# Depthwise weights behind the first outputs, urgency carried over table changes, and cross weights fetched later

## The chip, the cores and the metric

The program runs on the 8 NeuronCores of one Trainium2 chip; each core has TensorE (PE), VectorE (DVE), ScalarE (ACT), GpSimd (POOL) and SyncE (SP). The metric is the device time of the slowest core in microseconds. The input has 4 sequences of 4096 tokens; a core takes 2048 tokens of one sequence and 128 tokens ahead of them, the halo. There is no traffic between the cores.

## The reference, cut to what matters

```python
h = rmsnorm(x, norm_g)
(q, k, v, g_attn, u_conv, g_conv, q_cross, g_cross, merge) = split(h @ w_in)
a = sliding_window_attention(q, k, v, positions, attn_sinks)     # window 128, 8 heads
y_attn = (a * silu(g_attn)) @ w_o_attn
c = conformer_conv(u_conv, ...)       # GLU, causal depthwise conv of width 31, LayerNorm, silu
y_conv = (c * silu(g_conv)) @ w_pw + b_pw
m = memory_cross_attention(q_cross, rmsnorm(mem), w_mem_kv)      # 256 memory tokens, 4 heads
y_cross = (m * silu(g_cross)) @ w_o_cross
gates = sigmoid(merge)                # three gates per channel
x = x + (gates0 * y_attn + gates1 * y_conv + gates2 * y_cross) @ w_out
return rmsnorm(x, final_norm_g)
```

## The kernel before, in words

The 2048 tokens are four groups of 512 (tg 0 to 3) and sixteen blocks of 128 (B). Activations lie channel-major in SBUF, so most matmuls are 128x128 by 128x512, eight of them (k-chunks) to one projected unit of 128 channels. PSUM has eight banks of 512 float32.

**Stages.** (1) *Start*: x of group 0 arrives in eight chunks `xs0_0` to `xs0_7`. For each chunk ACT squares it and DVE multiplies it with the gain (`raw`, 128x512, bf16 out). Between the chunks DVE builds the attention's bias tiles from the positions (`bias_ops`, 128x128 operations). Then `rms_stats`, `rms_apply` (eight 128x512 scalar-tensor-tensor operations on DVE), and the units `u_k_raw`, four `u_q_raw` and `u_v`; DVE multiplies or copies each out of PSUM. (2) *Attention*, sixteen steps of a block: `scores` (banks 0 to 3, then four Exp on ACT), `att_l` (bank 5), `att_o` (bank 4), `att_r` (DVE, Ln and Exp on ACT, a 128x512 multiply on POOL), `att_g` (DVE, which empties bank 4). Each step has some projection units beside it (`fill`); a unit takes the next bank of `pj`, and must wait until what was in that bank has been read. (3) `glu_halo`, then the convolution stage: `glu` of group 0, `u_gc`, and per group `conv(c)` for c 0 to 3 with `glu` of the next group between them. `conv` reads `Rt`, a copy of the GLU result `aT` shifted per tap, written by 16 DMAs of SP per half group (`relayout(tg, cp)`: cp 0 serves conv 0 and 1, cp 1 serves conv 2 and 3). It also reads `Lw`, the depthwise weights spread on a diagonal, which POOL builds in 16 operations of 128x256 (`lw_part`). (4) Cross attention: `x_scores`, `x_attend`, `x_out`; its weights `w_qc` and `w_gx` come by two POOL DMAs of 1 MB each (bf16 in SBUF), first used when conv of the last group runs. (5) Merge and output projection.

**What sets the order.** `Prog.add` records every operation with reads and writes, a busy time, and for ACT the activation table. `Prog.plan` then makes each engine's order: PE and SP keep program order; ACT, DVE and POOL take, among the next 48, what can start first, and of those equally early the one with the least `due`. Due times go backwards from PE's. On ACT only operations of the current table group may be taken. Every engine runs its list in order, and waits for semaphores; an operation that waits holds up all behind it on its engine. DMAs of SP are "hardware_dynamic" in the profile, those of POOL "software_dynamic".

Since each helper issues its operation in one line, the profile's lines are those of helpers: L527 and L531 are matmuls (L531 the tiled ones of attention and convolution), L551 activations, L555 tensor-tensor, L566 and L569 tensor-scalar with one and two operations, L576 scalar-tensor-tensor, L580 copies, L588 DMAs.

Of the kernel before, what the change touches and what calls it, by code (L numbers as in the profile page):

```python
# [8 lines left out]
ALU = mybir.AluOpType  # L9
# [69 lines left out]
class Prog:  # L79
# [3 lines left out]
    RATE = {(True, False): (300e3, 0.0), (False, True): (0.0, 330e3), (True, True): (60e3, 260e3)}  # L83
# [70 lines left out]
    def plan(self):  # L154
# [14 lines left out]
        for op in reversed(ops):  # L169
            if op.eng != "pe":  # L170
                m = t + 10.0
                for u in users[op.idx]:
                    m = min(m, due[u])
                due[op.idx] = m - op.late - self.HOP - (2.0 if op.sem is not None else 0.0)
# [11 lines left out]
        free = {e: 5.0 for e in queue}  # L186
# [204 lines left out]
def build_program():  # L391
# [274 lines left out]
    def lw_part(cg):  # L666
        tt("pool", Lw[:, cg * 8:(cg + 1) * 8, :], E32.unsqueeze(1).to_broadcast([128, 8, 32]),
           consts[:, C_WR + cg * 8:C_WR + (cg + 1) * 8].unsqueeze(2).to_broadcast([128, 8, 32]), ALU.mult)
# [390 lines left out]
    def halo_stats():  # L1059
# [18 lines left out]
        [V(1), GA(1, 0), GA(1, 1), ST(2), AP(2, 0, 8)],  # L1078
# [3 lines left out]
        [V(2), GA(2, 0), GA(2, 1), load_conv],  # L1082
        [GA(2, 2), GA(2, 3), K(3), MQ(0, 8)],
# [3 lines left out]
        [GA(3, 3), MK(0), MK(1)],  # L1087
# [3 lines left out]
    pj[0] = [6, 7, 3]  # L1091
    for n in range(18):
        pjn[0] = 0
# [7 lines left out]
        first = 2 if n in (1, 5, 9) else 1  # L1101
        for f in here[:first]:
            f()
# [16 lines left out]
    glu(0, 0)  # L1120
    glu(0, 1)
# [9 lines left out]
    for tg in range(NTG):  # L1131
        nx = tg + 1
        for c in range(4):
            conv(c)
            if nx < NTG:
                glu(nx, c)
                if c % 2 == 1:
                    relayout(nx, c // 2)
            elif c < 2:
                u_qc(0, 2 * c)  # L1140
                u_qc(0, 2 * c + 1)
            else:
                u_gx(0, 2 * c - 4)
                u_gx(0, 2 * c - 3)
# [195 lines left out]
```

How the kernel before makes its waits and increments, by code:

```python
            def run(engname, e):  # L309
                seen = {}
                for i in order.get(engname, ()):
                    op = ops[i]
                    need = {}
                    for d in op.deps:
                        p = ops[d]
                        s = p.sem if p.sem is not None else p.eng
                        if p.sigval > need.get(s, 0):
                            need[s] = p.sigval
                    for s, v in need.items():
                        if seen.get(s, 0) >= v:
                            continue
                        e.wait_ge(sems[s], v)
                        seen[s] = v
                    ins = op.emit(e)
                    if op.signal:
                        s = op.sem if op.sem is not None else op.eng
                        ins.then_inc(sems[s], op.inc)
                if engname == "sp":
                    for fi in final_waits:
                        p = ops[fi]
                        s = p.sem
                        if seen.get(s, 0) < p.sigval:
                            e.wait_ge(sems[s], p.sigval)
                            seen[s] = p.sigval
```

## Time and profile before

| | before |
|---|---|
| median of 3 runs | 705.59 us (682.0 to 705.97) |
| the profiled execution | 681.28 us; span 679.7 us on core 4, the slowest; the eight cores 675.8 to 679.7 us |
| PE busy | 633.7 us, 93% |
| DVE, ACT, POOL busy | 347.7, 290.2, 121.6 us |
| DMA | 58.56 MB; software_dynamic 27.79 MB, hardware_dynamic 29.79 MB |

How to read it: nearly the whole span is PE work. What is not is found in PE's timeline, where an idle time stands in brackets in front of the instruction that ended it, with the engine that released it. A number behind "x" is a count. "PEclk" is the TensorE clock that was granted, as a share of 2.4 GHz; 0.50 is 1.2 GHz.

### The profile page before, as it was taken

The page shows a single profiled execution, that of the slowest core. Times are in us where ns is not written, and L with a number is a line of the kernel's source. Part 1 is how long each engine was busy: PE and PEld are TensorE (multiplying, and loading weights), DVE is VectorE, ACT ScalarE, POOL GpSimd, SP SyncE. Part 2 cuts the span into 40 slices and gives each one's busy share as a digit, 9 for nine tenths or more (in the row PEclk, how much of TensorE's full clock was granted, in tenths as well). Part 3 has the DMA queues.
Part 4 walks back from the last instruction along what each step waited for, and adds up shares of the span by engine and source line. Part 5 has one row for each costly group of instructions (what it writes and reads, how often), then busy time and mean ns, then how long its engine had stood idle before and what let it go on. Part 6 is the DMA issues. An engine that isn't in the chain of part 4 may idle for free.

```text
span 679.7 us, 11202 instructions; the slowest of 8 cores (675.8 to 679.7 us)
## 1 busy us (share of the span) xinstructions
PE 633.7 (93%) x3537; PEld 282.2 (42%) x3600; DVE 347.7 (51%) x570; ACT 290.2 (43%) x506; POOL 121.6 (18%) x155
## 2 busy tenths in 40 slices
PE   2499999997999999997999999999999999999994
PEld 0144434443444444443444444444444444444442
DVE  5989677754135453555565333344444343444336
ACT  4058865563236373657778322222222212222224
POOL 5301222121000000012322411122111222122210
PEclk9999999997999999998999999999999999999998
DMA  7895797005534233479900770210031002500003
GB/s 168 123 243 150 123 123 141 1 2 86 121 86 96 61 72 79 109 130 159 172 14 1 97 89 2 94 63 31 32 120 66 32 31 91 189 31 32 32 0 155
DMA packets 28281, 58.56 MB, mean 86 GB/s; under 512 B 3648, under 2 KB 17216, under 8 KB 26432
## 3 DMA queue, kind: packets, MB, share of 16 engines
q0 software_dynamic: 8624, 27.79, 23.4%
q1 hardware_dynamic: 19456, 29.79, 15.9%
q8 instruction: 31, 0.51, 0.3%
q14 instruction: 26, 0.21, 0.1%
q10 hardware_dynamic: 144, 0.26, 0.1%
HBM read 62.09 MB, written 8.39 MB: 104 GB/s over the span
## 4 chain that ended last, share of the span: by engine, by line
PE 84%; DVE 5%; issue 4%; ACT 3%; DMA 2%; SPq 2%; DVEq 0%; ACTq 0%
PE psum L527 75%; PE psum L531 9%; ACT arena L551 2%; DVE arena L555 2%; SPq L588 2%; DVE arena L566 2%; DVE arena L576 1%; DMA arena<-xT 1%; ACT L551 1%; DMA arena<-arena 0%; DVE arena L580 0%; DVE arena L569 0%; DVEq L322 0%; ACTq L322 0%; SPq L322 0%
## 5 line engine op out<-in xcount | busy, mean ns | idle before, releaser
L527 PE MATMUL psum<-arena 128*128 128x512 bf16 (+3 forms) x2705 | 570.3, 367 | 32.5 <-ACT arena L551 17.2
L527 PEld LDWEIGHTS psum<-arena 128*128 128x128 bf16 x2768 | 259.0, 98 | 342.9 <-issue 59.8
L551 ACT ACTIVATE arena<-psum 128x512 bf16<-128x512 f32 (+1 forms) x244 | 137.7, 597 | 231.8 <-PE psum L527 158.3
L555 DVE TENSOR_TENSOR arena<-psum,arena 128x512 f32<-128x512 f32 (+2 forms) x143 | 105.2, 745 | 133.1 <-PE psum L527 90.8
L555 POOL TENSOR_TENSOR arena<-arena 128x512 f32<-128x512 f32 (+3 forms) x95 | 96.3, 1020 | 282.5 <-DVE arena L576 152.8
L551 ACT ACTIVATE arena<-arena 128x512 f32<-128x512 f32 (+7 forms) x174 | 106.9, 643 | 91.2 <-DVE arena L555 71.0
L531 PE MATMUL psum<-arena 128*32 128x512 bf16 (+3 forms) x832 | 67.3, 383 | 4.5 <-DVE arena L555 2.4
L576 DVE SCALAR_TENSOR_TENSOR arena<-psum,arena 128x512 f32<-128x512 f32 (+2 forms) x52 | 37.0, 712 | 58.6 <-PE psum L527 55.4
L576 DVE SCALAR_TENSOR_TENSOR arena<-arena 128x512 bf16<-128x512 f32 (+4 forms) x79 | 60.8, 806 | 11.1 <-ACT arena L551 10.2
L580 DVE CAST arena<-psum 128x512 bf16<-128x512 f32 (+2 forms) x70 | 46.0, 660 | 35.1 <-PE psum L527 35.0
L551 ACT ACTIVATE arena<-psum,arena 128x512 bf16<-128x512 f32 (+4 forms) x58 | 35.7, 649 | 52.7 <-PE psum L531 31.4
L555 DVE TENSOR_TENSOR arena<-arena 128x512 bf16<-128x512 f32 (+3 forms) x78 | 44.6, 588 | 14.6 <-ACT arena L551 10.8
L531 PEld LDWEIGHTS psum<-arena 128*32 128x32 bf16 (+3 forms) x832 | 23.2, 99 | 45.1 <-issue 31.8
L588 POOL DMA_DIRECT2D arena<-win x11 | 6.1, 558 | 161.3 <-issue 124.9
L566 DVE TENSOR_SCALAR arena<-psum,arena 128x512 f32<-128x512 f32 x16 | 12.0, 751 | 39.2 <-ACT arena L551 38.1
L566 DVE TENSOR_SCALAR arena<-arena 128x128 bf16<-128x128 f32 (+5 forms) x58 | 22.4, 434 | 4.0 <-DMA arena<-xT 3.4
L551 ACT ACT_TABLE_LOAD x13 | 16.7, 1283 | 10.4 <-DVE arena L555 5.2
L569 DVE TENSOR_SCALAR arena<-arena 128x512 f32<-128x512 f32 (+3 forms) x33 | 10.9, 339 | 14.9 <-ACT arena L551 13.2
L555 DVE TENSOR_TENSOR arena<-arena,psum 128x512 f32<-128x512 f32 x16 | 10.3, 682 | 8.7 <-PE psum L527 8.7
L576 DVE SCALAR_TENSOR_TENSOR arena<-arena,psum 128x512 f32<-128x512 bf16 x16 | 11.0, 685 | 6.6 <-PE psum L527 5.3
L588 POOL DMA_DIRECT2D out<-arena x12 | 7.5, 626 | 28.6 <-DVE arena L576 26.6
L569 POOL TENSOR_SCALAR arena<-arena 128x1 f32<-128x1 f32 x12 | 2.3, 188 | 50.9 <-ACT arena L551 50.9
(14 smaller groups left out, 13.9 us busy)
## 6 DMA issues: line engine op xcount, KB each, us to landing
arena<-win POOLq DMA_DIRECT2D x11, 1024.0 KB, 16.0
arena<-xT SPq DMA_DIRECT2D x32, 256.0 KB, 7.8
arena<-xtok SPq DMA_DIRECT2D x16, 512.0 KB, 4.3
arena<-arena SPq DMA_DIRECT2D x96, 67.5 KB, 2.0
out<-arena POOLq DMA_DIRECT2D x12, 512.0 KB, 3.0
arena<-wo POOLq DMA_DIRECT2D x3, 1024.0 KB, 22.7
arena<-arena SPq DMA_DIRECT2D x32, 67.4 KB, 2.0
arena<-wqg POOLq DMA_DIRECT2D x4, 512.0 KB, 11.8
```

Of the source, the lines that this page charges most:

```text
L527: P.add("pe", lambda e: e.matmul(out, lhsT=lhsT, rhs=rhs, start=start, stop=stop), reads=[lhsT, rhs], writes=[out], busy=max(0.000421 * wi ...
L531: P.add("pe", lambda e: e.matmul(out, lhsT=lhsT, rhs=rhs, start=start, stop=stop, tile_position=tile_position), reads=[lhsT, rhs], writes= ...
L551: P.add("act", lambda e: e.activation(out=out, in_=in_, func=func, **kw), reads=rd, writes=wr, busy=0.06 + 0.00085 * width(out), lag=0.12, ...
L555: P.add(eng, lambda e: e.tensor_tensor(out=out, in0=in0, in1=in1, op=op), reads=[in0, in1], writes=[out], busy=vcost(eng, "tt", out, in_ps ...
L566: P.add(eng, lambda e: e.tensor_scalar(out=out, in0=in0, scalar1=s1, scalar2=None, op0=op0), reads=rd, writes=[out], busy=cost)
L569: P.add(eng, lambda e: e.tensor_scalar(out=out, in0=in0, scalar1=s1, scalar2=s2, op0=op0, op1=op1), reads=rd, writes=[out], busy=cost)
L576: P.add(eng, lambda e: e.scalar_tensor_tensor(out=out, in0=in0, scalar=scalar, in1=in1, op0=op0, op1=op1), reads=rd, writes=[out], busy=vc ...
L580: P.add(eng, lambda e: e.tensor_copy(out=out, in_=in_), reads=[in_], writes=[out], busy=vcost(eng, "copy", out, in_psum(in_)))
L588: P.add(eng, lambda e: e.dma_start(out=out, in_=in_), reads=[in_] + list(after), writes=[out], dsem=sem, final=final, busy=0.7 if eng == " ...
```

## The change

What it does:

- `lw_part` gets a read of the attention result of a block, so that it can only run after `att_g` of that block; the calls go from "one in each of steps 0 to 15" to steps 2 to 15 and two behind the loop.
- `plan`: the due time of an ACT operation is also bounded by the earliest due time of the next table group (`close`); SP is free from 6.5 instead of 5.0; the shares of bandwidth that it assumes for the two kinds of DMA (`RATE`) change.
- The units of the attention steps take banks 6 and 7 in turn, with no reset per step; before 6, 7 and 3, from 6 anew in each step. Some units are written in another order (`fill`).
- `att_o(15)` and `att_g(15)` come behind `glu(0, 0)`; `pjn` is set to 0 ahead of `glu_halo` alone, so the halo's four units take banks 6, 7, 0, 1 and `glu(0, 0)` takes 2 and 3. Before it was set to 0 again behind the halo, and `glu(0, 0)` took 6 and 7.
- The DMAs of `w_qc` and `w_gx` are issued after `conv(0)` of group 0 has written `cbf[:, 0, :]`; before ahead of `glu(0, 0)`.

```diff
-    RATE = {(True, False): (300e3, 0.0), (False, True): (0.0, 330e3), (True, True): (60e3, 260e3)}
+    RATE = {(True, False): (360e3, 0.0), (False, True): (0.0, 330e3), (True, True): (200e3, 160e3)}
...
+        close = {}
+        for op in reversed(ops):
+            if op.eng != "pe":
+                m = t + 10.0
+                for u in users[op.idx]:
+                    m = min(m, due[u])
+                due[op.idx] = m - op.late - self.HOP - (2.0 if op.sem is not None else 0.0)
+                if op.eng == "act":
+                    r = group[op.idx]
+                    due[op.idx] = min(due[op.idx], close.get(r + 1, m) - 1.3 - op.busy)
+                    close[r] = min(close.get(r, m), due[op.idx])
...
-        free = {e: 5.0 for e in queue}
+        free = {e: 6.5 if e == "sp" else 5.0 for e in queue}
...
-    def lw_part(cg):
...
+    def lw_part(cg, after):
+        e8 = E32.unsqueeze(1).to_broadcast([128, 8, 32])
...
+        P.add("pool", lambda e: e.tensor_tensor(out=out, in0=e8, in1=w8, op=ALU.mult), reads=[e8, w8, after], writes=[out],
+              busy=0.65)
...
-        [V(1), GA(1, 0), GA(1, 1), ST(2), AP(2, 0, 8)],
+        [GA(1, 0), V(1), GA(1, 1), ST(2), AP(2, 0, 8)],
...
-    pj[0] = [6, 7, 3]
-    for n in range(18):
-        pjn[0] = 0
+    pj[0] = [6, 7]
+    for n in range(17):
...
-        if n < 16:
-            lw_part(n)
+        if 2 <= n < 16:
+            lw_part(n - 2, part(gA, blocks[n - 2]))
...
-        if n == 16:
-            pj[0] = [6, 7, 0, 1, 2, 3]
-            glu_halo()
-
-    dma("pool", w_qc, win_d[3], "w3")
-    dma("pool", w_gx, win_d[4], "w4")
+    lw_part(14, part(gA, 13))
+    lw_part(15, part(gA, 13))
+    pj[0] = [6, 7, 0, 1, 2, 3]
+    pjn[0] = 0
+    glu_halo()
     glu(0, 0)
+    att_o(15)
+    att_g(15)
     glu(0, 1)
...
         for c in range(4):
             conv(c)
+            if tg == 0 and c == 0:
+                dma("pool", w_qc, win_d[3], "w3", after=[cbf[:, 0, :]])
+                dma("pool", w_gx, win_d[4], "w4")
```

**POOL's queue at the start.** The 128x256 operations are `lw_part`, the 128x512 ones `att_r`. Before:

```order
L588 DMA arena<-wkv 128x2048
L555 TENSOR_TENSOR arena<-arena 128x256 x10
L588 DMA arena<-wqg 128x2048 x4
L555 TENSOR_TENSOR arena<-arena 128x256 x5
L555 TENSOR_TENSOR arena<-arena 128x512 x2
L588 DMA arena<-wmem 128x8x512
```

and with the change:

```order
L593 DMA arena<-wkv 128x2048
L593 DMA arena<-wqg 128x2048 x4
L560 TENSOR_TENSOR arena<-arena 128x512
L675 TENSOR_TENSOR arena<-arena 128x256
L560 TENSOR_TENSOR arena<-arena 128x512
L675 TENSOR_TENSOR arena<-arena 128x256
L593 DMA arena<-wmem 128x8x512
```

No `lw_part` is left between the DMAs of the first weights; they stand among the multiplies of `att_r`. On DVE, 75 operations stood ahead of the first one of `rms_apply(0)` and 91 ahead of the last `u_q_raw(0)`; now 63 and 82: bias operations (128x128) that went behind.

**PE's queue from the last attention steps to the convolution.** The 128x30 rows are `glu_halo`, the four 64x512 behind them `att_o(15)`. Before:

```order
L531 MATMUL psum<-arena 64x512 x8
L527 MATMUL psum<-arena 128x30 x64
L531 MATMUL psum<-arena 64x512 x4
L527 MATMUL psum<-arena 128x512 x96
L531 MATMUL psum<-arena 32x512 x32
```

and with the change:

```order
L536 MATMUL psum<-arena 64x512 x8
L532 MATMUL psum<-arena 128x30 x64
L532 MATMUL psum<-arena 128x512 x16
L536 MATMUL psum<-arena 64x512 x4
L532 MATMUL psum<-arena 128x512 x80
L536 MATMUL psum<-arena 32x512 x32
```

`att_o(15)` went behind the sixteen matmuls of `glu(0, 0)`.

**DVE's queue where the last LayerNorm meets the first cross attention.** The x2 and x3 rows and the single arena<-arena ones are `ln_norm` (second step) and `ln_gate` of group 3, the CAST rows copy `u_qc` units, the L576 or L581 rows are `x_attend`. Before:

```order
L580 CAST arena<-psum 128x512
L555 TENSOR_TENSOR arena<-arena 128x512 x2
L580 CAST arena<-psum 128x512
L555 TENSOR_TENSOR arena<-arena 128x512 x2
L580 CAST arena<-psum 128x512
L576 SCALAR_TENSOR_TENSOR arena<-arena,psum 128x512
L555 TENSOR_TENSOR arena<-arena 128x512 x2
L580 CAST arena<-psum 128x512
L555 TENSOR_TENSOR arena<-arena 128x512
```

and with the change:

```order
L585 CAST arena<-psum 128x512
L560 TENSOR_TENSOR arena<-arena 128x512 x3
L585 CAST arena<-psum 128x512
L560 TENSOR_TENSOR arena<-arena 128x512
L585 CAST arena<-psum 128x512
L581 SCALAR_TENSOR_TENSOR arena<-arena,psum 128x512
L560 TENSOR_TENSOR arena<-arena 128x512 x3
```

The x2 behind the first copy was `ln_norm(1)` and `ln_gate(0)`, with `ln_norm(2)` in the next pair and `ln_norm(3)` in the third; the x3 is now `ln_norm(1)`, `(2)` and `(3)`, ahead of every `ln_gate`. In POOL's and SP's queues the two cross weights and the relayouts keep their places; what changes is what the first of the two weight DMAs waits for.

## Rows read from the trace of the kernel before

**Rows 1.** Page, part 1: busy us, share, instructions.

```profile
PE 633.7 (93%) x3537; PEld 282.2 (42%) x3600; DVE 347.7 (51%) x570; ACT 290.2 (43%) x506; POOL 121.6 (18%) x155
```

**Rows 2.** PE timeline: start, busy us, count, in brackets the idle time before.

```profile
26.38 0.58 PE L527 MATMUL psum<-arena 128*128 128x512 bf16 x1 [6.70 <-DVE arena L566]
...
41.05 0.61 PE L531 MATMUL psum<-arena 64*128 64x512 bf16 x4 [0.74 <-DVE arena L555]
```

**Rows 3.** Windows: length, busy of PE, PEld, DVE, ACT, POOL, clock, DMA.

```profile
10.20:22.50 12.30, 6.53 (x12) 1.33 (x12) 12.20 (x20) 5.96 (x10) 12.14 (x20) 1.00 0.69 162
22.50:31.70 9.20, 4.24 (x9) 1.28 (x10) 8.88 (x42) 0.00 (x0) 0.01 (x1) 1.00 0.99 149
```

**Rows 4.** Windows, columns as in rows 3.

```profile
60.00:153.00 93.00, 90.40 (x629) 40.32 (x636) 65.52 (x106) 61.11 (x117) 19.79 (x20) 1.00 0.52 80
...
159.90:165.10 5.20, 5.19 (x13) 1.88 (x13) 2.59 (x10) 0.98 (x2) 0.00 (x0) 0.50 0.86 132
...
314.60:320.00 5.40, 5.29 (x16) 1.99 (x17) 1.53 (x3) 3.62 (x7) 2.31 (x2) 0.68 0.97 152
```

**Rows 5.** PE timeline around `glu_halo` and `glu(0, 0)`.

```profile
156.31 0.62 PE L531 MATMUL psum<-arena 128*64 128x512 bf16 x4 [1.19 <-DVE arena L555]
159.91 23.36 PE L527 MATMUL psum<-arena 128*128 128x512 bf16 x94 [2.98 <-ACT arena L551]
```

**Rows 6.** Chain of waits, time and length of each step, `conv(0)` and `conv(2)`, group 0.

```profile
181.22 3.35 DMA arena<-arena
...
184.71 1.89 PE psum L531 x29
...
195.56 1.61 PE psum L531 x25
```

**Rows 7.** PE timeline where the cross attention starts.

```profile
314.60 7.73 PE L527 MATMUL psum<-arena 128*128 128x512 bf16 x26 [3.34 <-ACT arena L551]
```

**Rows 8.** DVE timeline (as rows 2): `ln_gate(2)` and the last `ln_norm(3)` of group 3.

```profile
310.62 1.02 DVE L555 TENSOR_TENSOR arena<-arena 128x512 bf16<-128x512 bf16 x2
```

**Rows 9.** ACT timeline where the cross attention starts.

```profile
312.56 1.28 ACT L551 ACT_TABLE_LOAD   x1
```

**Rows 10.** DVE timeline around the start.

```profile
31.75 5.38 DVE L576 SCALAR_TENSOR_TENSOR arena<-arena 128x512 bf16<-128x512 f32 x8
...
46.68 1.67 DVE L566 TENSOR_SCALAR arena<-arena 128x512 bf16<-128x512 f32 x4
```

**Rows 11.** POOL timeline and the wqg tile: its four DMAs, issue to landing.

```profile
17.40 2.20 POOL L588 DMA_DIRECT2D arena<-wqg  x4
...
DMA to landing us min/median/max: 7.0/11.8/16.6
```

**Rows 12.** DMA view, 196 to 198 us: issues, KB each, us to landing.

```profile
arena<-arena SPq DMA_DIRECT2D x2, 67.5 KB, 2.1
```

**Rows 13.** ACT timeline: `csq` and `cbf` of `conv(0)`, group 0.

```profile
186.70 1.27 ACT L551 ACTIVATE arena<-psum,arena 128x512 bf16<-128x512 f32 x2 [2.73 <-PE psum L531]
```

**Rows 14.** SP timeline: the sixteen DMAs of `relayout(0, 1)`.

```profile
182.03 11.40 SPq L588 DMA_DIRECT2D arena<-arena  x16
```

**Rows 15.** DMA view, 171.5 to 173.5 us: packets by queue, then issues.

```profile
q0 software_dynamic: 53, 0.43, 103.8%
...
arena<-arena SPq DMA_DIRECT2D x2, 67.5 KB, 3.8
```

**Rows 16.** The `out` tile: a store issued at 508.1, then one at 546.0 us.

```profile
DMA to landing us min/median/max: 5.4/5.4/5.4
...
DMA to landing us min/median/max: 3.0/3.0/3.0
```

**Rows 17.** The win tile (durations in ns) and the DMA view in slices of 0.4 us, 158 to 174.

```profile
L588 POOL DMA_DIRECT2D arena<-win x2: 538/566/594, 158.2 to 158.8; - x2
...
DMA to landing us min/median/max: 10.3/13.1/16.0
...
DMA  0000000593994999686999999999989839899894
```

More of the change, by code:

```diff
@@ L168, in plan @@
                 t += op.busy
[L169 to L174, printed above, removed]
         group = {}
@@ L664, in build_program @@
     dma("pool", w_ga[1], wqg_d[3], "w_ga1")
-    def lw_part(cg):
-        tt("pool", Lw[:, cg * 8:(cg + 1) * 8, :], E32.unsqueeze(1).to_broadcast([128, 8, 32]),
-           consts[:, C_WR + cg * 8:C_WR + (cg + 1) * 8].unsqueeze(2).to_broadcast([128, 8, 32]), ALU.mult)
+    def lw_part(cg, after):
+        e8 = E32.unsqueeze(1).to_broadcast([128, 8, 32])
+        w8 = consts[:, C_WR + cg * 8:C_WR + (cg + 1) * 8].unsqueeze(2).to_broadcast([128, 8, 32])
+        out = Lw[:, cg * 8:(cg + 1) * 8, :]
+        P.add("pool", lambda e: e.tensor_tensor(out=out, in0=e8, in1=w8, op=ALU.mult), reads=[e8, w8, after], writes=[out],
+              busy=0.65)
     ts("dve", hb2, ccol(C_BGLU + 4, 4), 0.5, ALU.mult)
@@ L1081, in build_program @@
         [Q(2, 2), Q(2, 3), ST(3), AP(3, 0, 8)],
-        [V(2), GA(2, 0), GA(2, 1), load_conv],
-        [GA(2, 2), GA(2, 3), K(3), MQ(0, 8)],
+        [GA(2, 0), V(2), GA(2, 1), load_conv],
+        [GA(2, 2), K(3), GA(2, 3), MQ(0, 8)],
         [Q(3, 0), mem_stats, Q(3, 1), Q(3, 2)],
@@ L1086, in build_program @@
         [GA(3, 1), lambda: normed(memn, memT, C_GM, rm), GA(3, 2)],
-        [GA(3, 3), MK(0), MK(1)],
+        [MK(0), GA(3, 3), MK(1)],
         [MK(2), MK(3), MV(0)],
@@ L1100, in build_program @@
             scores(blocks[n])
-        first = 2 if n in (1, 5, 9) else 1
-        for f in here[:first]:
+        for f in here:
             f()
@@ L1107, in build_program @@
             att_g(blocks[n - 2])
-        for f in here[first:]:
-            f()
-        if n < 16:
-            lw_part(n)
+        if 2 <= n < 16:
+            lw_part(n - 2, part(gA, blocks[n - 2]))
         if n == 14:
             clear_pads()
-        if n == 16:
-            pj[0] = [6, 7, 0, 1, 2, 3]
-            glu_halo()
-    dma("pool", w_qc, win_d[3], "w3")
-    dma("pool", w_gx, win_d[4], "w4")
+    lw_part(14, part(gA, 13))
[3 more added lines that the diff above has]
+    glu_halo()
     glu(0, 0)
+    att_o(15)
+    att_g(15)
     glu(0, 1)
```

## The prediction

> **What bounds the kernel now.** The page's first part says that PE is busy for 93% of the span [rows 1], and the change takes no matmul away; so I read PE's timeline for the idle times, and for each the chain of waits back to what was late. Five places matter. In all of them PE stands while a queue in a fixed order is behind.
>
> *Start.* PE waits 6.70 us until 26.38 for DVE's `raw` chunks, and `scores(1)` begins its second half at 41.05, again behind DVE [rows 2]. From 10.2 to 31.7 DVE is busy throughout, but while POOL runs `lw_part` it gets through 20 instructions in 12.30 us, and afterwards through 42 in 9.20 us [rows 3]. So this stretch is bound by DVE, and DVE is held by POOL.
>
> *Attention.* From 60 to 153 PE is busy 90.40 of 93 us; DVE has 27 us to spare, POOL 73 [rows 4].
>
> *GLU.* PE stands from 155.12 to 156.31 and then 2.98 us until 159.91 [rows 5]. The second wait is for bank 6, which the halo's first unit still holds. Then the matmuls run at a granted clock of 0.50, 1.2 GHz, until 165.10 [rows 4].
>
> *Convolution.* `conv(0)` starts at 184.71, released by the last relayout DMA [rows 6].
>
> *Cross attention.* PE waits 3.34 us for ACT until 314.60 [rows 7], and the next 5.40 us have a mean clock of 0.68 [rows 4]. The last `ln_norm` on DVE is in the pair from 310.62 [rows 8]; its activation and a table load of 1.28 us [rows 9] have to pass before the Exp.
>
> **The change, part by part.** The sum goes against the profiled execution, 681.28 us (span 679.7 and 1.6 around it). The median of the three runs shown is 705.59, 24.3 above it; their lowest, 682.0, agrees with it.
>
> 1. `lw_part` leaves the start. Free of POOL, DVE takes (9.20 - 4 x 0.42)/38 = 0.20 us for a 128x128 operation, with 0.42 for a 128x512 one from 1.67/4 [rows 3, 10]. The 20 held instructions (4 wide, 16 narrow, by this window's shapes) would take 4.9 instead of 12.3: 7.4 us less. Nine narrow operations go behind the last `u_q_raw`: 1.8 less. The four weight DMAs of POOL remain, 2.20 us of issue [rows 11], and fall into the same stretch; they can hold DVE for 0 to 2.2, I take 1.3. Result 7.9 us. Is anything else late next? These DMAs follow w_kv directly, about 3 us earlier than now; `w_q0` lands 7.0 after its issue at 17.40 [rows 11], at 24.4, so in the change at about 21.5, when `u_k_raw` (from 17.8, eight matmuls at 0.43) ends. x of group 1 moves by 3 us too and PE by 8, which uses up slack, perhaps 0.5. The eight `rms_apply`, 5.38 us [rows 10], stay. **-7.9** (bounds -10 and 0, if the DMAs decide).
>
> 2. Attention. The fifteen remaining `lw_part` of interest now hold DVE about 0.4 us each (12.30/20 less 0.20), 6 us of DVE's 27 spare. Each reads `gA`, so it can hold POOL, and behind it the next `att_r` multiply and `att_g`, only if `att_g` is late; one step lies between. Two banks instead of three: in a step of three units the third waits until the first is read, one unit of 1.7 us later; the Exp of a gate unit on ACT, behind four score Exps, is the slow one. Bank 3 no longer holds up `scores`. Together **+1.5** (bounds -1.5, half of PE's 2.6 idle, and +14, 1 us a step). SP's new 6.5 and the bandwidth shares act only in the plan: 0.
>
> 3. GLU. Halo matmuls end at 155.12; `glu(0, 0)` in banks 2 and 3 needs 16 x 0.216 = 3.5, `att_o(15)` 0.6: 159.2. Bank 6 was read at 159.91 even behind the stall, and bank 7 needs one more such read before it is wanted, eight matmuls later. Allowing 0.3, `glu(0, 1)` starts at 159.5 instead of 165.8 (159.91, 5.2 at half speed and four more matmuls). **-6.3** (bounds -3.7, if the clock falls anyway, and -6.6).
>
> 4. `relayout(0, 0)` no longer meets weights. The chain has 3.35 us from its last issue to `conv(0)` [rows 6], against a landing of 2.1 in quiet [rows 12]. **-0.6** (0 to -1.1).
>
> 5. Cross weights behind `cbf` of `conv(0)`. This is the large term. `cbf` is written at 187.97 [rows 13], and the sixteen DMAs of `relayout(0, 1)`, which `conv(2)` needs, are issued from 182.03 to 193.43, one in 0.66 to 0.71 [rows 14]. So the weights are issued with some eight of them still to come; their packets begin 2.8 us after issue, and relayout packets about 1.2 after theirs, so the last five or six arrive behind two megabytes. What happens then stands in the trace: three relayout DMAs were issued before 173.5 with the weights still moving, and from 171.5 to 173.5 all 53 packets were the weights' [rows 15]; they landed after 3.8 us instead of 2.1 [rows 12]. The reverse is seen too: a POOL store issued behind three SP loads lands after 5.4 us, one alone after 3.0 [rows 16]. What comes first is served first. The second weight, issued 0.6 after the first, lands 16.0 later: 16.6 us from the first issue, of which 2.8 pass before the first packet and 1.2 behind the last one, as for a relayout; that leaves 12.6 us of packets [rows 17]. Counted from C, the start of `conv(0)`: `cbf` C+3.3, first weight packet C+6.3, last C+18.8, remaining relayouts landed C+20.5. `conv(2)` is due at C+10.85 [rows 6]: a wait of 9.7. The clock then falls as after the wait at 159.91: 5.2/2 less matmuls already run, 2.2. **+11.9** (bounds 0, and +14.5). `relayout(1, 0)` is late next, but `conv(0)` of group 1 is 19.4 us behind `conv(2)`.
>
> The Trainium skill, "DMA: Bandwidth & Descriptors", section Queues, rings and completion order, says an engine takes turns between queue rows packet by packet, a packet being some 9 to 17 descriptors. The 2 us without a relayout packet agree with that only if a whole weight DMA is one packet. By that rule the relayouts would get a turn between the two weights; that is rival B.
>
> 6. Urgency over table changes. `ln_norm(2)` and `(3)` follow `(1)` directly (306.5 to 307.7), four Silu of 0.8 end at about 309.6, the table load at 310.9 [rows 9], one Exp at 311.5; PE is there at 311.26 (314.60 - 3.34) [rows 7]. The wait shrinks from 3.34 to 0.3, and the low clock goes: (1 - 0.68) x 5.40 = 1.7 [rows 4]. **-4.7** (bounds 0 and -5.0).
>
> Sum: -7.9 + 1.5 - 6.3 - 0.6 + 11.9 - 4.7 = -6.1, so 675.2.
>
> **The rivals.**
>
> A (forecast), chance 0.50: 675.2, from 669 to 682 by the small terms.
>
> B, 0.15: the relayouts slip in between the two weights. Then they wait for one, 6.3 us less, and the clock may hold, 1 less: 668. For it: two separate DMAs. Against it: five relayouts of four descriptors per DMA engine need several turns.
>
> C, 0.15: no hold-up. Small packets interleave with the weights, or the last relayouts are out before them: 675.2 - 11.9 = 663.3. For it: at 173.5 the weights' rest was short, so a long hold-up is not seen. Against it: the served-first rows [rows 15, 16].
>
> D, the other side, 0.10: the attention steps pay for two banks and for POOL. Place: the third unit of a step, on PE, behind DVE's copy and ACT's Exp of the first. From 0.6 us a step this eats the forecast's gain (14 steps, 8 us); at 1 us it gives 675.2 - 1.5 + 14 = 687.7, and with the low clock after larger waits up to 696. For it: DVE is 70% busy there and gets 6 us more. Against it: before, PE lost only 2.6 us there.
>
> E, 0.08: the start does not get shorter, as first weights and x bound it: 683. For it: DMA share 0.99 from 22.5 [rows 3].
>
> 0.02 is left for something else.
>
> **The numbers.** Predicted 675. The cases reach from 663 (C) to 688 (D) with 0.9 of the chance. An execution like the two runs at 705.6 to 706.0 would put the forecast at 675 x 1.036 = 699; no row prices that difference and a median may lie there, so the high end is 700; for an execution like the profiled one the range is 662 to 688. Faster by over 2% is below 667.7, on equal footing: C, half of B and a little of A, 0.28. Slower by over 2%, above 694.9: the far end of D and what is left, 0.04. Within 2% (about what a measurement of this kernel can tell from no change): 0.68.
>
> **What would show it.** (1) Half of `scores(1)` at about 33 instead of 41.05. (2) PE idle over 0.5 us in attention at few steps. (3) `glu(0, 0)` directly behind the halo, clock 1.00. (5) A wait of some 9.7 us before `conv(2)` of group 0, released by a relayout DMA with a landing time over 10 us, then a clock of 0.50. Without it the forecast is wrong by its largest term and C holds. (6) No wait over 1 us between `x_scores(0)` and `x_scores(2)`. The forecast is also wrong if the first weights land no earlier.

## The result: 0.4% faster

| | before | changed |
|---|---|---|
| median of 6 runs | 694.03 us (681.68 to 795.22) | 678.85 us (677.0 to 679.52) |
| ratio of the times | | 0.9957, 95% interval 0.9942 to 0.9971 |
| profiled execution, span of the slowest core | 679.7 us | 677.8 us (the cores 671.1 to 677.8) |

The medians differ by more than the ratio, since some runs of the kernel before were disturbed; the ratio leaves those out. It is a gain of 2.9 us, 2 to 4 by the interval. The time forecast was 675 (675.2 in its sum). Against the profiled execution of before that was a gain of 6.1 us, twice what came.

**Where it came from and went.** From the traces of all eight cores the start of each unit's first weight load was read; the table has the median of the cores, in us, and the difference to before.

| start of | before | changed | difference | forecast so far |
|---|---|---|---|---|
| scores(1) | 39.5 | 31.1 | -8.4 | -7.9 |
| last u_q_raw of group 1 | 64.9 | 60.3 | -4.6 | |
| glu_halo | 152.9 | 146.9 | -6.0 | -6.4 |
| glu(0, 3) | 171.3 | 159.7 | -11.6 | -12.7 |
| conv(2), group 0 | 193.4 | 181.9 | -11.5 | -13.3 |
| conv(3), group 0 | 198.8 | 201.3 | +2.4 | -1.4 |
| x_scores(0) | 300.2 | 302.8 | +2.6 | -1.4 |
| x_scores(3) | 317.0 | 315.2 | -1.8 | -6.1 |
| end of the span | 677.2 | 675.4 | -1.8 | -6.1 |

So 11.5 us were won by conv(2) of group 0, 13.9 lost there, and 4.4 won in the cross attention. These are two single executions, and their 1.8 is not the 2.9 of the ratio; the table is for the places, the ratio for the total.

### The profile page after: what moved, and what is told of

It reads as the page before. It is cut to its first block, busy times and chain, and to the rows that moved or that the text cites. A ratio compares the mean times of both kernels' runs of the same rounds, so it can differ in the third digit from the quotient of the medians.

```text
span 677.8 us, 11291 instructions; the slowest of 8 cores (671.1 to 677.8 us)
## 1 busy us (share of the span) xinstructions
PE 635.3 (94%) x3600; PEld 280.2 (41%) x3600; DVE 344.9 (51%) x570; ACT 289.4 (43%) x506; POOL 122.7 (18%) x155
## 4 chain that ended last, share of the span: by engine, by line
PE 76%; DMA 6%; DVE 6%; SPq 4%; issue 4%; ACT 2%; POOL 1%; DVEq 0%; ACTq 0%; POOLq 0%
PE psum L532 70%; PE psum L536 7%; SPq L593 4%; DVE arena L581 3%; DMA arena<-xT 2%; DMA arena<-arena 2%; DMA arena<-wqg 2%; DVE arena L560 2%; ACT arena L556 2%; DVE arena L585 1%; POOL arena L560 1%; ACT L556 0%; POOL arena L593 0%; DVEq L327 0%; DVE arena L574 0%
## 5 line engine op out<-in xcount | busy, mean ns | idle before, releaser
L532 PE MATMUL psum<-arena 128*128 128x512 bf16 (+2 forms) x2768 | 571.3, 366 | 20.9 <-ACT arena L556 14.5
L560 POOL TENSOR_TENSOR arena<-arena 128x512 f32<-128x512 f32 (+2 forms) x79 | 85.1, 1078 | 250.6 <-DVE arena L581 185.5
L581 DVE SCALAR_TENSOR_TENSOR arena<-arena 128x512 bf16<-128x512 f32 (+4 forms) x79 | 65.4, 864 | 6.5 <-ACT arena L556 5.2
L581 DVE SCALAR_TENSOR_TENSOR arena<-psum,arena 128x512 f32<-128x512 f32 (+2 forms) x52 | 37.0, 712 | 58.1 <-PE psum L532 54.6
L560 DVE TENSOR_TENSOR arena<-arena 128x512 bf16<-128x512 f32 (+3 forms) x78 | 43.3, 571 | 12.7 <-ACT arena L556 9.2
L571 DVE TENSOR_SCALAR arena<-arena 128x128 bf16<-128x128 f32 (+5 forms) x58 | 16.9, 334 | 9.0 <-DMA arena<-xT 8.2
L675 POOL TENSOR_TENSOR arena<-arena 128x256 bf16<-128x256 bf16 x16 | 12.0, 756 | 24.8 <-DVE arena L560 24.7
L574 DVE TENSOR_SCALAR arena<-arena 128x512 f32<-128x512 f32 (+3 forms) x33 | 10.1, 316 | 11.8 <-ACT arena L556 10.1
L560 DVE TENSOR_TENSOR arena<-arena,psum 128x512 f32<-128x512 f32 x16 | 10.3, 679 | 8.7 <-PE psum L532 8.7
L581 DVE SCALAR_TENSOR_TENSOR arena<-arena,psum 128x512 f32<-128x512 bf16 x16 | 10.9, 684 | 4.2 <-PE psum L532 2.8
## 6 DMA issues: line engine op xcount, KB each, us to landing
arena<-wqg POOLq DMA_DIRECT2D x4, 512.0 KB, 12.3
```

The source lines that it names most:

```text
L532: P.add("pe", lambda e: e.matmul(out, lhsT=lhsT, rhs=rhs, start=start, stop=stop), reads=[lhsT, rhs], writes=[out], busy=max(0.000421 * wi ...
L560: P.add(eng, lambda e: e.tensor_tensor(out=out, in0=in0, in1=in1, op=op), reads=[in0, in1], writes=[out], busy=vcost(eng, "tt", out, in_ps ...
L571: P.add(eng, lambda e: e.tensor_scalar(out=out, in0=in0, scalar1=s1, scalar2=None, op0=op0), reads=rd, writes=[out], busy=cost)
L574: P.add(eng, lambda e: e.tensor_scalar(out=out, in0=in0, scalar1=s1, scalar2=s2, op0=op0, op1=op1), reads=rd, writes=[out], busy=cost)
L581: P.add(eng, lambda e: e.scalar_tensor_tensor(out=out, in0=in0, scalar=scalar, in1=in1, op0=op0, op1=op1), reads=rd, writes=[out], busy=vc ...
L675: P.add("pool", lambda e: e.tensor_tensor(out=out, in0=e8, in1=w8, op=ALU.mult), reads=[e8, w8, after], writes=[out], busy=0.65)
```

## The profile of the changed kernel

The page's first part and four windows, columns as in [rows 3]; core 6, the slowest, as in every view of this kernel here.

```profile
PE 635.3 (94%) x3600; PEld 280.2 (41%) x3600; DVE 344.9 (51%) x570; ACT 289.4 (43%) x506; POOL 122.7 (18%) x155
```

```profile
10.20:22.50 12.30, 8.19 (x18) 2.04 (x18) 12.19 (x51) 5.40 (x9) 2.76 (x5) 1.00 1.00 204
22.50:31.70 9.20, 9.16 (x73) 4.84 (x73) 8.87 (x23) 0.00 (x0) 0.00 (x0) 1.00 1.00 175
60.00:153.00 93.00, 89.65 (x680) 40.13 (x680) 66.93 (x100) 58.50 (x111) 30.45 (x35) 1.00 0.46 71
195.40:201.20 5.80, 5.26 (x34) 1.90 (x35) 0.22 (x1) 1.27 (x2) 0.00 (x0) 0.50 0.46 114
```

Against [rows 3]: DVE, busy for as long, now gets 51 instructions through in the first 12.3 us instead of 20, while POOL has 5 instead of 20. The engine that looked saturated was being held (e5 below moves `lw_part` alone and shows it). The fourth window is new: the clock at 0.50, 1.2 GHz, behind a long wait.

PE's timeline, which answers to [rows 2], [rows 5] and [rows 7]: start, busy us, count, and in brackets the idle time.

```profile
31.09 1.16 PE L536 MATMUL psum<-arena 64*64 64x512 bf16 x12
...
154.23 17.43 PE L532 MATMUL psum<-arena 128*128 128x512 bf16 x80 [0.35 <-DVE arena L581]
...
194.56 0.58 PE L536 MATMUL psum<-arena 128*32 128x512 bf16 x1 [11.03 <-DMA arena<-arena]
195.94 3.57 PE L536 MATMUL psum<-arena 128*32 128x512 bf16 x29 [0.79 <-DMA arena<-arena]
...
314.69 354.43 PE L532 MATMUL psum<-arena 128*128 128x512 bf16 x1640 [0.35 <-ACT arena L556]
```

The waits of 2.98 us at the halo and 3.34 at the cross attention are gone; from 314.69 the timeline has one row to the end. In their place stand 11.8 us in front of conv(2) (11.03 and 0.79; over the cores 8.2 to 11.0 and 0.8 to 1.0). The 29 matmuls that follow take 3.57 us, where in a quiet place they take 1.89.

The chain of waits there (start, us, what), which answers to [rows 6], and the DMA view of four stretches of 2 us, as [rows 15]: 173 to 175, 178 to 180, 187 to 189 and 195 to 197.

```profile
181.25 0.70 SPq L593
181.95 0.04 issue
181.99 13.38 DMA arena<-arena
195.38 0.56 issue
```

```profile
q1 hardware_dynamic: 164, 0.14, 29.5%
...
q0 software_dynamic: 31, 0.25, 97.2%
...
q0 software_dynamic: 37, 0.29, 92.2%
q1 hardware_dynamic: 36, 0.03, 5.4%
...
q1 hardware_dynamic: 627, 0.54, 111.4%
```

The last relayout DMA that conv(2) needs lands 13.38 us after its issue, against 2.1 in quiet [rows 12]. The four stretches tell why. Alone, and at the pace of SP's issue, the relayouts (q1) have 164 packets in 2 us. When the weights (q0) begin, at 177.5, no relayout packet starts for 2.8 us (1.6 to 5.1 over the cores); no run shows why. Then one relayout packet passes for each weight packet, 36 to 37. But a weight packet has 8 KB and a relayout packet 0.9 (0.29 MB/37, 0.03/36), so relayouts run at 18 packets a us. When the weights are out, at 193.0, the backlog of `relayout(0, 1)` and `relayout(1, 0)` drains at over 300 a us, and conv(2) goes on 3.0 us later (2.9 to 3.3 over the cores).

## The experiments

Each ratio is to the kernel before in the same session. "e1" is the base for several. The differences of starts are medians of the eight cores.

**e1_w_group1.** The cross weights one group later.

```diff
-            if tg == 0 and c == 0:
+            if tg == 1 and c == 0:
                 dma("pool", w_qc, win_d[3], "w3", after=[cbf[:, 0, :]])
```

> The changed kernel with one edit: the two cross weights are issued behind conv(0) of group 1 instead of group 0; every queue keeps its order. Theory T (the packets of the weights hold back the relayout DMAs that conv(2) of group 0 needs): the wait of 11.8 us before conv(2) and the low clock behind it go, relayout landings there fall from about 10 us to 2.1, and the time is 678.9 - 13.9 = 665.0, ratio to before 0.975. The weights then meet relayout(2, 0), which has some 9 us to spare. Rival R (relayout(0, 1) is late by itself, because the GLU ended 5.6 us earlier and SP needs 0.65 us for each of 32 DMAs): a wait of 2 us or more stays at conv(2) and the time is 668 or above.

Measured: 666.17 us, ratio 0.9757 (0.9738 to 0.9776). conv(2) on core 1:

```profile
184.10 1.89 PE L536 MATMUL psum<-arena 128*32 128x512 bf16 x29 [0.54 <-DMA arena<-arena]
```

The wait of 11.8 us is 0.54, with nothing moved but the weights' DMAs, and with e3 the hold-up is shown both ways. This version beats both kernels.

**e3_before_cbf.** That edit alone in the kernel before.

```diff
-    dma("pool", w_qc, win_d[3], "w3")
-    dma("pool", w_gx, win_d[4], "w4")
...
             conv(c)
+            if tg == 0 and c == 0:
+                dma("pool", w_qc, win_d[3], "w3", after=[cbf[:, 0, :]])
+                dma("pool", w_gx, win_d[4], "w4")
```

> The kernel before with one edit: the two cross weights issued behind cbf of conv(0) of group 0, as in the change. Theory T: five relayout DMAs are left when the weight packets start, a wait of about 10.5 us before conv(2) and 2.2 of low clock: +12.5 us, 694.3, ratio 1.018. relayout(0, 0) meets no weights any more, up to 0.6 less. Rival R (the hold-up is there only because the GLU stage ended earlier): a wait under 5 us and a time under 688.

Measured: 696.05 us, ratio 1.020 (1.0179 to 1.0222). By conv(3) 13.9 us are lost, in spite of all else being as before; the waits are 8.5 to 11.1 us, and 0.8 to 1.1 behind the first matmul. On core 6, `glu(0, 0)` and conv(2):

```profile
161.16 23.67 PE L527 MATMUL psum<-arena 128*128 128x512 bf16 x96 [2.60 <-DVE arena L576]
...
205.83 0.58 PE L531 MATMUL psum<-arena 128*32 128x512 bf16 x1 [9.87 <-DMA arena<-arena]
```

The first row bears on the GLU: the wait behind the halo is there with no weight moving near it.

**e2_split8.** Smaller packets, same bytes, same place.

```diff
-                dma("pool", w_qc, win_d[3], "w3", after=[cbf[:, 0, :]])
-                dma("pool", w_gx, win_d[4], "w4")
+                for kc in range(KC):
+                    dma("pool", w_qc[:, kc, :], win_d[3][:, kc, :], "w3_%d" % kc, after=[cbf[:, 0, :]])
+                for kc in range(KC):
+                    dma("pool", w_gx[:, kc, :], win_d[4][:, kc, :], "w4_%d" % kc)
```

> The changed kernel with each of the two cross-weight DMAs cut into eight by k-chunk, in the same place; a packet then has 1 KB instead of 8 KB. In the changed kernel's trace about as many relayout packets of 0.9 KB as weight packets of 8 KB start while both queues have work (43 to 43, 37 to 36, 38 to 40 in 2 us). Theory V (the engines take one packet of each queue in turn, so that the size of the weights' packets sets the relayouts' rate): about 70 relayout packets a us instead of 20, the nine relayout DMAs still to come when the weights start (700 packets) need some 10 us, the wait before conv(2) falls from 11.8 to about 5 us, the time to about 672. Rival Q (what was issued first is served first, whatever its packets): the wait stays at 11 to 12 us and the time at 679. If packets keep 8 KB all the same, nothing changes either, and the sizes in the DMA view will tell.

Measured: 674.01 us, ratio 0.9876 (0.9857 to 0.9896). The DMA view from 184 to 186 us and PE at conv(2), core 2:

```profile
q0 software_dynamic: 317, 0.29, 88.9%
q1 hardware_dynamic: 167, 0.15, 27.0%
```

```profile
185.33 0.38 PE L536 MATMUL psum<-arena 128*32 128x512 bf16 x1 [1.66 <-DMA arena<-arena]
189.71 3.41 PE L536 MATMUL psum<-arena 128*32 128x512 bf16 x29 [4.01 <-DMA arena<-arena]
```

The weights move as many bytes in 2 us (0.29 MB), yet 84 relayout packets a us pass instead of 18, and the wait is 5.7 us instead of 11.8 (4.4 to 6.7 over the cores against 9.1 to 11.8). So packets of both queues take turns, and their size decides what each gets. One thing else differs: the issue of sixteen DMAs is spread over 8.8 us, from 176.35 on, with relayouts issued between them, and by first come, first served that would let these through early too. But the last weight DMA is issued at 184.6, and the relayouts issued from 186 to 188 land after 5.9 us, while weight packets go on until 195. First come, first served, on which the forecast stood, is refuted by that, and plainest by e9 below. The turns were two to one here and not one to one; why is open.

**e14_half.** w_gx goes to group 1, w_qc stays.

```diff
                 dma("pool", w_qc, win_d[3], "w3", after=[cbf[:, 0, :]])
+            if tg == 1 and c == 0:
-                dma("pool", w_gx, win_d[4], "w4")
+                dma("pool", w_gx, win_d[4], "w4", after=[cbf[:, 0, :]])
```

> The changed kernel with w_qc behind conv(0) of group 0 and w_gx behind conv(0) of group 1: one megabyte at the place of the hold-up instead of two. Theory V: until the weight's last packet, near C+13, about 20 relayout packets a us, some 150 of 700; the other 550 need 2 us more and 1 to land, while conv(2) is due at C+11: a wait of 4 to 5 us instead of 11.8 and the low clock behind it, 671.4 in all, ratio 0.984. Rival (the wait comes from having two weight DMAs in the queue, or from the issue itself, rather than from their length): it stays above 8 us, or it is gone.

Measured: 672.43 us, ratio 0.9867 (0.9848 to 0.9886), with 5.3 us of waits on the slowest core (3.6 to 5.6 over all); 671.4 and 4 to 5 us were expected. The wait ends 3.5 to 4.1 us after the last weight packet, in the changed kernel 2.9 to 3.3: how long the weights move sets its end, with half of them as with all.

**e4_w_early.** The weights ahead of glu(0, 0), as in the kernel before.

```diff
+    dma("pool", w_qc, win_d[3], "w3")
+    dma("pool", w_gx, win_d[4], "w4")
     glu(0, 0)
     att_o(15)
...
-            if tg == 0 and c == 0:
-                dma("pool", w_qc, win_d[3], "w3", after=[cbf[:, 0, :]])
-                dma("pool", w_gx, win_d[4], "w4")
```

> The changed kernel with the two cross weights issued ahead of glu(0, 0), where they were before. Theory T: no wait over 1 us at conv(2), and conv(0) starts up to 1.5 us later, as relayout(0, 0) meets the weights: 665 to 667. On the GLU term: if the banks and att_o(15) are what made glu(0, 0) start directly behind the halo, it still does and the clock stays at 1.00. Rival G (the weights' transfers had slowed the halo's readers, and their absence is what helped): a wait of some 3 us behind the halo and a clock of 0.50 come back, 670 or more.

Measured: 672.64 us, ratio 0.9858 (0.9841 to 0.9875), slower than either theory had it, by something that neither saw. The weights are written over an area that att_o(15) still reads; here it reads what they wrote (so block 15 of the attention is another), and PE waits for them, on core 4:

```profile
160.05 1.06 PE L536 MATMUL psum<-arena 128*64 128x512 bf16 x4 [6.74 <-DMA arena<-win]
```

That is why the two moves of the change belong together. On the GLU the run tells nothing, for glu(0, 0) starts at 148.9 and the first weight DMA is issued at 148.72 on core 4, with its first packets near 151.0: nothing moved yet when glu(0, 0) began. That the transfers are not what held it is shown by e3 and e7, where the wait stands without them.

**e9_w_glu1.** The weights at the earliest place that is allowed.

```diff
     att_g(15)
+    dma("pool", w_qc, win_d[3], "w3")
+    dma("pool", w_gx, win_d[4], "w4")
     glu(0, 1)
...
-            if tg == 0 and c == 0:
-                dma("pool", w_qc, win_d[3], "w3", after=[cbf[:, 0, :]])
-                dma("pool", w_gx, win_d[4], "w4")
```

> The changed kernel with the cross weights issued right behind att_g(15), ahead of glu(0, 1): the earliest place at which nothing still reads the area they are written to. Theory V (a turn each, so a relayout packet of 0.9 KB per weight packet of 8 KB): weight packets from about 161 to 174 us, relayout(0, 0) is served at 20 packets a us until then and needs about 1250; it lands near 178.5, conv(0) starts 6 us later than 172, and relayout(0, 1), issued behind it, lands in time for conv(2). With a fall of the clock behind the wait 6 to 8 us more than e1: 672 to 674, ratio 0.986. Rival Q' (relayouts that are issued after the weights get their share of the bandwidth): conv(0) at most 2 us later, 668 or less.

Measured: 669.42 us, ratio 0.9802 (0.9781 to 0.9823): between the two expectations. conv(1) is 3.3 us further behind conv(0) than in e1, spread over several short waits, and the mean clock stays at 0.995. Two stretches of the DMA view, core 0, where relayouts are issued from 162.02: 164 to 166 and 170 to 172.

```profile
q0 software_dynamic: 44, 0.29, 104.6%
...
q0 software_dynamic: 49, 0.40, 95.8%
q1 hardware_dynamic: 48, 0.04, 7.4%
```

This is the pattern on which the forecast was built [rows 15], seen in full: for over 4 us after their issue the relayouts have no packet at all, then they have every second one, although both weight DMAs had been issued by 157.6, ahead of every relayout. The forecast took the silence for the rule. What the silence itself comes from is open; turns alone would not give it.

**e7_glu_back.** e1 with att_o(15) and the banks of glu(0, 0) as before.

```diff
     glu_halo()
+    att_o(15)
+    att_g(15)
+    pjn[0] = 0
     glu(0, 0)
-    att_o(15)
-    att_g(15)
```

> The changed kernel with the cross weights behind conv(0) of group 1 (e1), and att_o(15), att_g(15) and the banks of glu(0, 0) as before: att_o(15) ahead of glu(0, 0), which takes banks 6 and 7. No weight is transferred near the halo. Theory (banks and att_o(15) are the GLU term): PE waits 1.2 us before att_o(15) and some 3 us for bank 6, the clock falls to 0.50: 5.6 us more than e1, 671.8, ratio 0.984. Rival G (it was the weights' transfers): no wait, the time stays at 666.2.

Measured: 670.88 us, ratio 0.9828 (0.9813 to 0.9844). On core 4:

```profile
155.37 22.94 PE L532 MATMUL psum<-arena 128*128 128x512 bf16 x96 [2.60 <-DVE arena L581]
```

The wait for bank 6 is back with no weight moving. From glu_halo to glu(0, 3) e7 takes 17.7 us, e1 12.8. That is the term: 4.9 us here, 5.6 between the two kernels. The banks and the place of att_o(15) were put back together, so what each gives alone is not shown.

**e5_before_lw.** Only lw_part moved, in the kernel before.

```diff
+    def lw_part(cg, after):
...
-        if n < 16:
-            lw_part(n)
+        if 2 <= n < 16:
+            lw_part(n - 2, part(gA, blocks[n - 2]))
...
+    lw_part(14, part(gA, 13))
+    lw_part(15, part(gA, 13))
```

> The kernel before with one edit: lw_part reads the attention result of a block and runs behind att_g, as in the change. On DVE all but two operations keep their places, so the nine bias operations are still ahead of rms_apply. Theory (POOL's lw_part slows DVE in the start): the twenty held DVE operations take 4.9 us instead of 12.3, less 1.3 for the weight DMAs; scores(1) starts 6.1 us earlier (8.4 in the changed kernel, the rest being the nine operations). About 2.4 of it is given back by step 5, as in the changed kernel, because x of group 1 arrives no earlier: 678.8, ratio 0.994. Rival (the first weights and x bound the start): scores(1) less than 2 us earlier, time 681 or above.

Measured: 678.66 us, ratio 0.9947 (0.9932 to 0.9963). scores(1) starts 8.0 us earlier, where 6.1 was expected, so nearly all of the start's gain is lw_part's; but the halo starts only 3.3 us earlier.

**e10_lw_back.** The reverse, from e1.

```diff
-        if 2 <= n < 16:
-            lw_part(n - 2, part(gA, blocks[n - 2]))
+        if n < 16:
+            lw_part(n)
...
-    lw_part(14, part(gA, 13))
-    lw_part(15, part(gA, 13))
```

> e1 with lw_part back in its place of before (one call in each step, which the planner puts between the first weights' DMAs). In the kernel before, moving it alone gave 8.0 us at scores(1) but 3.3 at the halo. If what is given back is the price of x of group 1, which is the same with everything else in place: scores(1) 8 us later, the halo 3 to 4, time 669.7, ratio 0.981. Rival (in the changed order nothing is given back): the halo 6 to 7 us later, 673, ratio 0.986.

Measured: 669.01 us, ratio 0.9821 (0.9802 to 0.9841); e1, run again beside it (e11_group1_again), 664.15 and 0.9751 (0.9732 to 0.977). That is 4.9 us; scores(1) is 6.1 later and the halo 5.2. It lies between the two theories: less is given back here than in e5.

**e11_group1_again.**

> The kernel of e1 again (the change with the cross weights behind conv(0) of group 1), as the base for the three kernels beside it. 666, ratio 0.9757 as before.

It repeated, and gives the spread: up to the halo e1, e11, e9, e7 and the changed kernel are the same program, and the halo starts at 146.1, 145.5, 147.3, 148.6 and 146.9 (e14 145.3, e2 147.4). A difference in attention under 3 us between two profiles says little; there the timed ratios and single waits have to speak.

**e8_three_banks.** e1 with three banks for the attention's units.

```diff
-    pj[0] = [6, 7]
+    pj[0] = [6, 7, 3]
     for n in range(17):
+        pjn[0] = 0
```

> e1 with the three unit banks 6, 7, 3 of the kernel before, from 6 anew in each step, instead of 6 and 7 in turn; the fill lists stay as changed. The prediction had put two banks at +1.5 us: then this kernel is 1 to 1.5 us faster than e1 (ratio 0.974). Rival (bank 3 being also the scores' fourth bank, sharing it costs more than a third bank gives; in the traces the attention from step 8 to the halo lost nothing with two banks): 1 to 3 us slower than e1, ratio 0.978 to 0.980.

Measured: 667.29 us, ratio 0.9799 (0.9776 to 0.9822), 3.1 us slower than e11. On core 4, in scores(9):

```profile
101.59 1.60 PE L536 MATMUL psum<-arena 64*64 64x512 bf16 x7 [1.76 <-ACT arena L556]
```

scores uses banks 0 to 3. Its last part has to wait until ACT has read bank 3, which the third unit of the step before, u_ga(2, 1), had filled. The halo is only 2.4 us later, within the spread, but the ratio's intervals don't meet: two banks are a gain, not a loss, with the units in the order of the change.

**e6_before_close.** Only the urgency, in the kernel before.

```diff
...
+                if op.eng == "act":
+                    r = group[op.idx]
+                    due[op.idx] = min(due[op.idx], close.get(r + 1, m) - 1.3 - op.busy)
+                    close[r] = min(close.get(r, m), due[op.idx])
```

> The kernel before with one edit: the due times of ACT's operations are bounded by the next table group's (close). Theory: ln_norm(2) and (3) follow (1), the wait of 3.34 us between x_scores(0) and (2) and the low clock behind it go, nothing else moves: 4.4 us less, 678.1, ratio 0.9935. Rival (the order at the cross attention came from the other planner numbers or from the banks): nothing changes there, ratio 1.000.

Measured: 677.12 us, ratio 0.9923 (0.9907 to 0.9938), 4.4 us between x_scores(0) and (3). PE at the place of the 3.34 us [rows 7]:

```profile
312.31 17.91 PE L532 MATMUL psum<-arena 128*128 128x512 bf16 x81 [0.34 <-ACT arena L556]
```

**e12_x1_early, e13_x1_free, e15_x1_free_b, e16_xh_behind.** Four, all from e1, on what gives back part of the start's gain. They change when x of group 1 is released, what the raw chunks of group 1 read, and what is loaded first. In e13 and e15 these chunks read x of group 0, which is there already, so the result of group 1 is not the reference's; they are for the time alone.

```diff
-    dma("sp", xh, xh_d, "xh", after=[w_ga[0]])
+    dma("sp", xh, xh_d, "xh", after=[w_q[1]])
```

> e1 with the loads of xh and of x of groups 1 and 2 released by the landing of w_q[1] instead of w_ga[0]. Theory X (after the start PE is 8 us ahead, x of group 1 only 3, and its raw chunks are what gives back 3.8 us by u_q_raw of group 1): the chunks come 2 to 3 us earlier and 1 to 2.5 us of the loss go: 664.5, ratio 0.973. Rival (the DMA engines are full in this stretch, share 1.0, so what x gains w_ga loses, and u_ga(0, 0) waits for it instead): no gain or up to 2 us slower, ratio 0.976 to 0.979.

Measured: 666.19 us, ratio 0.9778 (0.9759 to 0.9798), 2.0 us slower than e11. scores(2) comes 2.9 us later, but not for the rival's reason: PE has no wait for w_ga on any core. ACT's queue now has the first square of x of group 1 ahead of the four Exp of scores(1). On core 0 that square waits for x until 35.33, the Exp start at 35.87 (33.19 in e11), and PE stands 1.66 us behind them; seven of the eight cores have such a wait, 0.6 to 1.8 us. In e11 the square waits for x until 36.27, but there it stands behind the Exp. x came hardly earlier, and a queue in a fixed order passed its wait on to PE.

```diff
-            act(hT[bi][:, kc, :], xs[bi][:, kc, :], AF.Square)
-            ts("dve", xg[bi][:, kc, :], xs[bi][:, kc, :], ccol(C_GX + kc), ALU.mult)
+            act(hT[bi][:, kc, :], xs[0][:, kc, :], AF.Square)
+            ts("dve", xg[bi][:, kc, :], xs[0][:, kc, :], ccol(C_GX + kc), ALU.mult)
```

> e1 with the raw chunks of group 1 (squares and products) computed from x of group 0, which is there already, so that they don't wait for x of group 1; the result of group 1 is not the reference's, rms_apply(1) still reads the right x. Theory X (the arrival of x of group 1 gives back the start's gain): u_q_raw(1, 3) starts 2 to 4 us earlier than in e1, near 57, and the time is 662 to 664, ratio 0.972. Rival (DVE and ACT are the bound there, whatever arrives): less than 1 us, 665, ratio 0.975.

Measured: 673.14 us, ratio 0.9859 (0.9821 to 0.9897). The expectation did not foresee that the loads of x of group 2 write the same buffer and stand ahead: the chunks waited for them instead. On core 4 ACT began them at 45.80 us and PE waited 5.03 us; u_q_raw(1, 3), the last of group 1, came at 64.0 instead of 59.3. With these loads behind the chunks:

```diff
     xload(1)
-    xload(2)
...
-        [GA(0, 2), GA(0, 3), lambda: squares("act", hTh, xh), RAW(2, 8)],
+        [GA(0, 2), GA(0, 3), lambda: squares("act", hTh, xh), RAW(2, 8), lambda: xload(2)],
```

> As e13 (e1 with the raw chunks of group 1 computed from x of group 0, so that group 1's result is not the reference's), with the loads of x of group 2 moved behind these chunks, so that nothing has to arrive for them. Theory X (the arrival of x of group 1 gives back the start's gain): u_q_raw(1, 3) starts 2 to 4 us earlier than in e1 (59.3 to 60.2), less up to 1 for the chunks' DVE operations that now fall into the start; time 662 to 664, ratio 0.971 to 0.973. Rival (DVE or ACT is the bound there whatever arrives): under 1 us earlier, ratio 0.975.

Measured: 663.07 us, ratio 0.9721 (0.9693 to 0.9749). u_k_raw(1) comes at 44.5, 9.3 us earlier than in the kernel before, so up to there nothing of the gain is given back. u_q_raw(1, 3) comes at 57.5, in e11 at 59.3 and in e1 at 60.2. So the arrival of x of group 1 takes 1.8 to 2.7 of what is given back; that is not far outside the spread, for e1, e11, e9, e14, e2 and the changed kernel reach this unit between 59.3 and 61.0. Some 2 us more go between u_k_raw(1) and u_q_raw(1, 3), for a cause that no run shows.

```diff
-    dma("sp", xh, xh_d, "xh", after=[w_ga[0]])
-    xload(1)
+    xload(1, [w_ga[0]])
+    dma("sp", xh, xh_d, "xh")
...
-        [halo_stats, lambda: normed(hTh, xh, C_GX, rstdh), ST(1), AP(1, 0, 8), lambda: u_k_raw(1, xg[1]), u_halo, QR(0)],
+        [ST(1), AP(1, 0, 8), lambda: u_k_raw(1, xg[1]), halo_stats, lambda: normed(hTh, xh, C_GX, rstdh), u_halo, QR(0)],
```

> e1 with x of group 1 loaded ahead of xh (0.5 MB, some 2 us of full DMA engines) and rms_stats(1), rms_apply(1), u_k_raw(1) ahead of the halo's statistics. Theory X: the raw chunks come up to 2 us earlier, 1 to 1.5 us of what is given back goes; 663.5, ratio 0.973. Rival (u_halo and the halo's statistics then come late, and PE waits for them instead): no gain or slower, 0.975 to 0.978.

Measured: 668.17 us, ratio 0.9804 (0.9776 to 0.9833). x does come earlier: DVE's last raw chunk of group 1 starts at 41.3 and 41.4 on cores 0 and 4 (42.4 to 45.1 on these cores of e1 and e11), and u_k_raw(1) at 44.9 instead of 46.8. But then the rival has it, PE waits for the halo's operations, on core 0:

```profile
51.66 1.31 PE L532 MATMUL psum<-arena 128*128 128x128 bf16 x5 [2.62 <-DVE arena L581]
```

and the last u_q_raw of group 1 starts at 63.5. What is loaded first comes first, and what stands behind it comes later: neither order of these loads that was tried makes the kernel faster than e1.

## Why the prediction was half right

The time is 0.6% above the forecast and within A, but the gain, 2.9 us of 6.1, is less than half of what was forecast. At five of the six places the trace moved the way that was forecast, though not always for the forecast's reason, and at the fourth nothing moved; the sizes were off by 4.3 us in sum by the table, and all but the start were off to the side of less gain.

1. *Start*, -7.9 forecast, -8.4 measured. e5 shows that lw_part does it (8.0 alone). Its parts fit less well: the forecast had 7.4 - 1.3 = 6.1 for lw_part with the weight DMAs and 1.8 for nine operations that go behind. e5, without these nine, has 8.0, e10 6.1, so 0.4 to 2.3 are left for the nine and all else, and in part the sum came right by errors that cancel.
2. *Attention*, +1.5 forecast, +2.4 measured, for the wrong reasons. "Two banks instead of three" was priced as a cost; e8 shows a gain of some 3 us. And the slack that x of group 1 would use up, "perhaps 0.5" in step 1 and not in its sum, is 3.8 us by the last u_q_raw of group 1, about half of it the arrival of x (e15); 1.4 of it is won back by the halo. DVE's timeline of the changed kernel has it, the first and the last of four waits for these chunks:

```profile
37.07 0.49 DVE L571 TENSOR_SCALAR arena<-arena 128x512 bf16<-128x512 f32 x1 [2.19 <-DMA arena<-xT]
...
43.99 0.49 DVE L571 TENSOR_SCALAR arena<-arena 128x512 bf16<-128x512 f32 x1 [1.70 <-DMA arena<-xT]
```

   [rows 3] already had the DMA engines at 0.99: a stretch that is shortened in front of full engines ends when they have brought what it needs.
3. *GLU*, -6.3 forecast, -5.6 measured. glu(0, 0) stands directly behind the halo, as forecast; e7 has the cause.
4. *relayout(0, 0)*, -0.6 forecast, none measured. PE's wait for the last relayout is 0.38 us now, but over the median of the cores conv(0) and what follows come no earlier.
5. *Cross weights*, +11.9 forecast, +13.9 measured. This is the step that failed most, in size and in mechanism. The wait itself was forecast at 9.7, and came at 10.3 (median of the cores); what is left of the 13.9, 3.6 us, goes to the slow clock, forecast at 2.2: the matmuls of conv(2) run one by one between landings, the 29 that follow take 1.7 us more than in a quiet place, and the unit behind them up to 0.8. "What comes first is served first" was wrong: e2 and the packet counts show turns. That the number nearly held is luck: with packets of nine to one in size, turns look like a queue, and by either rule the relayouts land just behind the last weight packet. The Trainium skill, "DMA: Bandwidth & Descriptors", section Queues, rings and completion order, had turns packet by packet, and the changed kernel's counts agree (36 to 37). Those of e2, 317 to 167, do not, if the turns are even and the packets that the profile counts are those of the page; no run shows whether they are. The forecast set it aside over two microseconds in [rows 15], and concluded that a whole weight DMA would have to be one packet. They fit the silence behind an issue that e9 shows in full, and say nothing of what follows it.
6. *Urgency*, -4.7 forecast, -4.4 measured; e6 alone gives it.

Rival B had the turn between the two weights, which is the wrong unit. C had the mechanism right, that small packets pass between the weights', and the price wrong: at 18 packets a us the hold-up stays. D fell with the sign of e8, E with e5.

## What to carry to other kernels

Ask of a large transfer that is moved behind the first use of a buffer not whether it is late but what small DMAs are still to be issued then, and how large its packets are: here a queue of 0.9 KB packets next to one of 8 KB got a tenth of the bytes. Here one line, the weights one group later, were worth 13 us, where the whole change brought 2.9. A gain ahead of full DMA engines should be priced to the next arrival, not to the end. A shared bank is to be looked at from both of its users. And an operation that waits for a load may stand ahead of another that PE needs, as in e12.

## What was not expected of the hardware

- Two DMA queues with work share the engines by packets: 36 to 37 in 2 us with 0.9 and 8 KB. With weight packets of 0.9 KB it was 167 to 317.
- Relayout DMAs that are issued while a queue of 8 KB packets runs have no packet for more than 4 us (e9), against a whole landing of 2.1 us in quiet.
- DVE's operations of 128x128 between POOL's lw_part: 20 instructions in 12.30 us; without them 51, in the same busy time.
